# A ninth block-product pair for the first head pair's queries and keys, and the convolution's norm spread over units and value tiles

## The chip, the cores and the metric

One core of one Trainium2 chip runs the whole layer as one program. The metric is the device time of one launch in microseconds (us), the median of several launches; lower is better. Engines are named as in the profile: PE (matrix multiply; PEld is its weight load), DVE (vector), ACT (scalar), POOL (GpSimd), SP (queues most transfers).

## The reference, cut to what matters

One encoder layer over 1024 tokens of width 1024, in float32, output (1, 1024, 1024):

```python
proj = x @ w_in[l] + b_in[l]                      # 1024 x 4608: GLU input | q | k | v | branch gates
glu_in, q, k, v, gate_logits = jnp.split(proj, splits, axis=-1)
# conv_branch
u = a * jax.nn.sigmoid(gate)                      # then a causal depthwise conv of width 31
u = jax.nn.silu(layer_norm(u, ln_g, ln_b))        # layer norm over the 512 channels
y_conv = u @ w_out
y_attn = chunked_attention(heads(q), heads(k), heads(v), rel_bias[l]) @ w_attn_out[l]   # 8 heads of 64
g_conv, g_attn = jnp.split(jax.nn.sigmoid(gate_logits), N_BRANCHES, axis=-1)
mixed = (g_conv * y_conv + g_attn * y_attn) @ w_o[l] + b_o[l]
x = layer_norm(ALPHA * x + mixed, ...)            # then a grouped mixture of 16 experts, top 2, and a last norm
```

## The kernel before, in words

Every float32 product is made from three passes over operands that are split in a high and a low part (`mm3`, L685 to L687). ACT makes the high part of a weight block (`high`), POOL or DVE the low part (`low`). Channels lie on partitions, tokens along the free axis; a block is 128 output channels.

The work of PE runs through these stages, in the order of the PE program:

1. **GLU blocks** 0 to 7 (`weights_left`). Beside them DVE makes the GLU (`glu`) and the first of 124 convolution taps (`conv_tap`, each 128x1024 in the PSUM banks 6 and 7); SP loads the first unit weights into slots of the ring as blocks are used up (`load_unit`).
2. **Units.** The 16 gate blocks are made in 8 pairs (a block of conv gates and one of attention gates). A pair is a 2x2 product of halves (tokens in 2 halves of 512, input channels in 2 halves of 512), and seven block products stand in for eight (`UNITS`, `gate_product`, order `1, 6, 5, 7, 2, 3, 4`). A unit is 12 matmuls of 512 columns into one of six banks, 56 units in all. Four of the seven products of a pair need sums of weight halves: POOL issues those as transfers that accumulate in DRAM (`sums_round`, `weight_sums`), in rounds; the rounds 5 and 6 stand after the low part of units 4 and 9 (`LATE_ROUNDS`). DVE adds the products into `gst` (`gate_sums`, 7 sums a pair) and does one or two taps between them. ACT does the sigmoids and SP stores the gates. A unit waits until the bank of the unit six before it has been read (`bank_read`).
3. **Conv mean and value tiles.** `conv_mean` (L745) sums the channels by a matmul with ones. Then 8 value tiles for heads 0 to 3 (24 matmuls of 256 columns each) in four banks, with `conv_var` (L753) ahead of tile 5. On DVE: `centre` (L1367, 4 times), `square_sum`, and `v_low` (L1354) of each tile, which needs ACT's `v_high` (L1084) of that tile; then four reciprocals (L1376) and four `normalise` (L1349). ACT: four squares, `v_high`, a square root, the high parts of two blocks, four Silu (L1111).
4. **Queries and keys of the first head pair**: blocks 10 and 11, 96 matmuls of 512 columns into banks 0 to 3; ACT and DVE turn them into `qh`, `ql`, `kh`, `kl` (`qk_high`, `qk_low`).
5. **Attention**, 32 slots (`scores_of_slot`, `weigh_values`), with the queries and keys of the later head pairs and the rest of the values in between; then the output products, the norm and the experts, which the diff doesn't touch.

All engines run their programs in order. POOL's order in stage 3 is: low parts of blocks 8 to 11, two bias scalings (`scale_bias`, L609), low parts of blocks 12 and 13, then attention.

Of the kernel before, what the change touches and what calls it, by code (L numbers as in the profile page):

```python
# [39 lines left out]
VAR_TILE = 5  # L40
CCE_ROW = 2048
FIRST_UNITS = 4
LATE_ROUNDS = {4: 5, 9: 6}
# [6 lines left out]
B_V = (8, 16)  # L50
B_Q = (10, 12, 14, 18)
B_OC, B_OA, B_WO = 20, 24, 28
N_BLOCKS = 36
W_GATE = N_BLOCKS

# [9 lines left out]
UNITS = [(x, q) for q in range(KC) for x in ORDER]  # L65
N_UNITS = len(UNITS)
GATES_STORED = 16 * KC // 2


def block_columns():  # L70

    a, g, q, k, v, gate = 0, 4, 8, 12, 16, 20
    cols = []
    for j in range(CB):
        cols += [a + j, g + j]
    cols += [v, v + 1, q, k, q + 1, k + 1, q + 2, k + 2, v + 2, v + 3, q + 3, k + 3]
    return cols, [gate + j for j in range(N_GATE)]
# [21 lines left out]
def encoder_layer(nc, xT, x, wblk, b_in, dw, dwb, lncg, lncb, relb, b_o, ln1_g, ln1_b,  # L99
# [3 lines left out]
    wsum_dram = nc.dram_tensor("gate_weight_sums", (4, KC, P * DC), F32, kind="Internal").ap()  # L103
    gate_dram = nc.dram_tensor("gate_cols", (N_GATE, P, SEQ), F32, kind="Internal").ap()
    ctx = ExitStack()
    with ctx:
# [197 lines left out]
        def wait_used(eng, n):  # L304
# [3 lines left out]
            elif n < B_V[0]:  # L308
                eng.wait_ge(blk_used, B_V[0] + N_UNITS - 2 * (B_V[0] - 1 - n))
            elif n in B_V or n - 1 in B_V:  # L310
                eng.wait_ge(v_done, TT * (1 + (n >= B_V[1])))
            elif n < B_OC:
                b, i = [(b, n - B_Q[b]) for b in range(PAIRS) if 0 <= n - B_Q[b] < 2][0]
                eng.wait_ge(qk_done, 1 + max(p for p in range(4 * PAIRS) if qk_of(p)[:2] == (b, i)))
# [17 lines left out]

        def sum_round(x, q):

            return q // 2 + {5: 1, 7: 1, 6: 2, 3: 3}[x]

        def sums_issued(r):

            return sum(2 * many for g in range(KC // 2) for stage, many in enumerate((4, 2, 1, 1)) if g + stage <= r)
# [15 lines left out]
        def sigmoids_at(m):  # L355
# [3 lines left out]
            x, q = UNITS[m - 2]  # L359
            return [(q, slot) for after, slot in ((7, 3), (2, 0), (3, 2), (4, 1)) if after == x]  # L360
# [7 lines left out]
        V_BANKS = (0, 1, 2, 3)  # L368
# [53 lines left out]
        SPLITS = {1: (14,), 2: (15,), 5: (16,), 9: (17,), 13: (18,), 17: (19,), 25: (20,), 27: (21,), 29: (22,), 30: (23,),  # L422
                  31: (24,), 32: (25,), 33: (26,)}
# [41 lines left out]
        with nc.Block() as block:  # L465
            @block.sync
            def _(sp):
# [17 lines left out]
                def load_unit(m):  # L485

                    x, q = UNITS[m]
                    if m < UNIT_SLOTS:
                        sp.wait_ge(blk_used, B_V[0] - RING + m // 2 + 1)
# [5 lines left out]
                    sp.dma_start(uraw[:, m % UNIT_SLOTS], of.rearrange("(p k c) -> p k c", p=P, k=CB)).then_inc(u_in[m % UNIT_SLOTS], 16)  # L495
# [30 lines left out]
                for m in range(N_UNITS):  # L526
                    if m + UNIT_SLOTS < N_UNITS:
                        load_unit(m + UNIT_SLOTS)
                    elif m % 2:
# [8 lines left out]
                for n in range(B_V[0] + RING, B_WO):  # L538
# [4 lines left out]
                    if n == B_OA - 2:  # L543

                        sp.wait_ge(qk_done, 4 * PAIRS)
# [36 lines left out]
            def _(pool):  # L582
# [38 lines left out]
                def weight_sums(g, stage):  # L621

                    if not 0 <= g < KC // 2:
                        return
                    for q in (2 * g, 2 * g + 1):
# [10 lines left out]
                def sums_round(r):  # L636
# [3 lines left out]
                    for stage in range(4):  # L640
                        weight_sums(r - stage, stage)

                def unit_low(m):

                    s = m % UNIT_SLOTS
# [37 lines left out]
            def _(pe):  # L683
# [34 lines left out]
                def gate_product(m):  # L718

                    x, q = UNITS[m]  # L720
                    s, bank = m % UNIT_SLOTS, unit_bank(m)
# [26 lines left out]
                def conv_var():  # L748
                    bank_read(N_UNITS - 2)
                    bank_read(N_UNITS - 1)  # L750
                    pe.wait_ge(sum_ok, 2 * (CB - 1))
                    for h in range(2):
                        last = pe.matmul(ps[:, 4 + h, :], ones[:], sqr[:, 0, HALF * h:HALF * h + HALF], start=True, stop=True)  # L753
# [140 lines left out]
                def qk_sum(p, part, between=None, first=3):  # L894

                    b, i, h = qk_of(p)
                    if part == 0:
                        pe.wait_ge(w_lo, B_Q[b] + i + 1)
                        if p == 5:
                            pe.wait_ge(cent, CB)  # L900
                        elif p not in (4, 15):
# [114 lines left out]
            def _(act):  # L1016
# [11 lines left out]
                def unit_high(m):  # L1028
                    act.wait_ge(u_in[m % UNIT_SLOTS], 16 * (m // UNIT_SLOTS + 1))
                    act.activation(uh[:, m % UNIT_SLOTS], uraw[:, m % UNIT_SLOTS], ACT.Copy).then_inc(u_hi, 1)  # L1030
# [38 lines left out]

                for m in range(N_UNITS + 2):  # L1070
# [6 lines left out]
                    for q, slot in sigmoids_at(m):  # L1077
                        gate_sigmoid(q, slot)

# [6 lines left out]
                def qk_high(i, o):  # L1086
# [4 lines left out]
                    act.wait_ge(qk_done, i + 1)  # L1091
                    act.activation(dst[:, HALF * h:HALF * h + HALF], o, ACT.Identity,
                                   bias=b_in_t[:, col:col + 1]).then_inc(qk_hi, 1)

                for j in range(CB):
                    act.wait_ge(cent, j + 1)
                    act.activation(sqr[:, j, :], cv[:, j, :], ACT.Square).then_inc(sq_done, 1)
                for t in range(TT):
                    v_high(0, t, ps[:, V_BANKS[t % 4], 0:2 * P])
                    if t == 1:  # L1100
                        high(B_Q[0])
                    if t == 3:
                        high(B_Q[0] + 1)
                    if t == VAR_TILE:
                        act.wait_ge(stat_done, 2)
                        act.activation(std[:], psf[:, 4 * HALF:6 * HALF], ACT.Sqrt, scale=1.0 / DC, bias=eps[:]).then_inc(sq_done, 1)
                high(B_Q[1])
                high(B_Q[1] + 1)
                for j in range(CB):
                    act.wait_ge(nrm, j + 5)  # L1110
                    act.activation(cv[:, j, :], cv[:, j, :], ACT.Silu, scale=cpar[:, 1, j:j + 1],  # L1111
                                   bias=cpar[:, 2, j:j + 1]).then_inc(silu_done, 1)
                for i in range(4):
                    qk_high(i, ps[:, i, :])
# [96 lines left out]
            def _(dve):  # L1211
# [49 lines left out]
                def first_low(m):  # L1261
                    dve.wait_ge(u_hi, m + 1)
                    dve.tensor_tensor(ul[:, m], uraw[:, m], uh[:, m], ALU.subtract).then_inc(u_lo, 1)
# [45 lines left out]

                sums_made = [0]  # L1310
# [29 lines left out]
                glu(CB - 1)  # L1340
# [3 lines left out]
                assert taps == CB * CW  # L1344
# [11 lines left out]
                def qk_low(i, o):  # L1356
# [5 lines left out]
                    dve.scalar_tensor_tensor(out=lo[b % 2][:, c], in0=o, scalar=b_in_t[:, col:col + 1],  # L1362
                                             in1=hi[b % 2][:, c], op0=ALU.add, op1=ALU.subtract).then_inc(qk_lo, 1)

                dve.wait_ge(stat_done, 1)
                for j in range(CB):
                    dve.scalar_tensor_tensor(out=cv[:, j, :], in0=psf[:, 6 * HALF:8 * HALF], scalar=-1.0 / DC, in1=cv[:, j, :],  # L1367
                                             op0=ALU.mult, op1=ALU.add).then_inc(cent, 1)
# [1094 lines left out]
```

## Time and profile before

| what | value |
| --- | --- |
| time before, median of 3 runs | 1120.44 us (1118.47 to 1121.39) |
| time of the profiled execution | 1120.55 us |
| its span | 1118.8 us, granted clock 0.987 on average |
| PE, DVE, ACT, POOL busy | 97%, 74%, 50%, 33% of the span |
| units, from the first to the last | 95.4 to 253.6 us |
| conv mean and value tiles | 254.9 to 281.6 us |
| first queries and keys | 282.6 to 304.5 us |

A row of the timeline reads: start, duration, engine, line, operation, output <- inputs, shape, xcount (rows of one kind that follow each other are merged), and in brackets the idle time before it with what ended it. Durations of matmuls overlap: the time from one start to the next is the pace.

### The profile page before, as it was taken

The page shows a single profiled execution, that of the slowest core. Times are in us where ns is not written, and L with a number is a line of the kernel's source. Part 1 is how long each engine was busy: PE and PEld are TensorE (multiplying, and loading weights), DVE is VectorE, ACT ScalarE, POOL GpSimd, SP SyncE. Part 2 cuts the span into 40 slices and gives each one's busy share as a digit, 9 for nine tenths or more (in the row PEclk, how much of TensorE's full clock was granted, in tenths as well). Part 3 has the DMA queues.
Part 4 walks back from the last instruction along what each step waited for, and adds up shares of the span by engine and source line. Part 5 has one row for each costly group of instructions (what it writes and reads, how often), then busy time and mean ns, then how long its engine had stood idle before and what let it go on. Part 6 is the DMA issues. An engine that isn't in the chain of part 4 may idle for free.

```text
span 1118.8 us, 17230 instructions
## 1 busy us (share of the span) xinstructions
PE 1081.1 (97%) x5487; PEld 897.1 (80%) x5488; DVE 833.2 (74%) x1195; ACT 556.9 (50%) x854; POOL 365.0 (33%) x317
## 2 busy tenths in 40 slices
PE   9999999999999999999999999899999999999984
PEld 7887888888788889788888888788888888888762
DVE  7899999995667766666774688888588646548766
ACT  6412343434476755645330224487487545548764
POOL 2535454444176854667000000024122121112220
PEclk9998999999999999999999999999999999999998
DMA  9898555543201100450750435898999975699966
GB/s 324 252 232 192 162 161 147 159 145 104 75 20 43 31 33 7 183 225 23 269 188 1 157 149 204 304 329 313 377 325 365 317 250 183 205 382 327 348 206 243
DMA packets 60938, 222.68 MB, mean 199 GB/s; under 512 B 9169, under 2 KB 9553, under 8 KB 56770
## 3 DMA queue, kind: packets, MB, share of 16 engines
q1 hardware_dynamic: 51602, 182.49, 44.0%
q0 software_dynamic: 9264, 39.27, 14.5%
q8 instruction: 40, 0.66, 0.2%
q14 instruction: 32, 0.26, 0.1%
HBM read 189.27 MB, written 49.30 MB: 213 GB/s over the span
## 4 chain that ended last, share of the span: by engine, by line
PE 81%; DVE 6%; DMA 4%; ACT 3%; issue 3%; POOL 2%; DVEq 1%; ACTq 0%; SPq 0%; POOLq 0%
PE ps L685 15%; PE ps L687 15%; PE ps L686 15%; PE ps L1823 8%; PE ps L1825 8%; PE ps L1824 8%; PE ps L807 2%; PE ps L793 2%; DMA dn_raw<-in_wexp 2%; DMA gu<-in_wexp 2%; PE ps L779 2%; PE ps L1904 1%; PE ps L1819 1%; POOL pr L597 1%; PE ps L1931 1%
## 5 line engine op out<-in xcount | busy, mean ns | idle before, releaser
L1722 DVE TENSOR_TENSOR gu<-gu (+1 forms) x128 | 148.5, 1219 | 34.7 <-issue 20.8
L1245 DVE SCALAR_TENSOR_TENSOR ps<-u,dw_t,ps 128x1024 f32<-128x1024 f32 x116 | 149.1, 1285 | 2.3
L1823 PE MATMUL ps<-gu,xgh 128*128 x336 | 134.0, 399 | 3.4 <-DVE xgl L2221 2.8
L1716 ACT ACTIVATE gu<-gu (+1 forms) x128 | 124.0, 1047 | 21.7 <-DMA gu<-in_wexp 13.6
L1825 PE MATMUL ps<-gu,xgl 128*128 x336 | 131.7, 392 | 0.0
L1824 PE MATMUL ps<-gu,xgh 128*128 x336 | 131.4, 391 | 0.0
L597 POOL TENSOR_SCALAR pr<-pr,rinv 128x640 f32<-128x640 f32 (+4 forms) x64 | 95.4, 1503 | 77.3 <-DVE rinv L1407 77.1
L685 PE MATMUL ps<-xh,wh 128*128 128x512 f32 x256 | 102.9, 402 | 1.7 <-DVE vhl L1354 1.0
L686 PE MATMUL ps<-xl,wh 128*128 128x512 f32 x256 | 100.0, 390 | 0.0
L687 PE MATMUL ps<-xh,wl 128*128 128x512 f32 x256 | 99.8, 390 | 0.0
L647 POOL TENSOR_TENSOR ul<-uraw,uh 128x512 fp32r<-128x512 f32 x52 | 68.6, 1436 | 71.4 <-ACT uh L1030 71.4
L2316 DVE TENSOR_TENSOR dn_l<-dn_raw,dn_h 128x1024 fp32r<-128x1024 f32 x60 | 69.5, 1219 | 10.9 <-ACT dn_h L2064 10.8
L1823 PEld LDWEIGHTS ps<-gu,xgh 128*128 128x128 f32 x336 | 63.4, 189 | 17.4 <-issue 4.8
L1825 PEld LDWEIGHTS ps<-gu,xgl 128*128 128x128 f32 x336 | 63.4, 189 | 13.5
L1824 PEld LDWEIGHTS ps<-gu,xgh 128*128 128x128 f32 x336 | 63.6, 189 | 12.7
L1823 PE MATMUL ps<-dn_h,hbh 128*128 128x512 f32 x168 | 68.3, 407 | 2.4 <-DVE hbl L2320 2.4
L1760 POOL DMA_INDIRECT acc_rows<-ys,to_now x20 | 37.6, 1880 | 94.0 <-ACT ys L2089 77.6
L1825 PE MATMUL ps<-dn_h,hbl 128*128 128x512 f32 x168 | 66.6, 397 | 0.0
L1824 PE MATMUL ps<-dn_l,hbh 128*128 128x512 f32 x168 | 66.5, 396 | 0.0
L1120 ACT ACTIVATE pr<-pr,nmx 128x640 f32<-128x640 f32 (+4 forms) x64 | 44.1, 690 | 43.8 <-DVE nmx L1398 43.8
L1747 POOL COPY id_now<-ids_i 128x1 int32 (+1 forms) x19 | 11.3, 594 | 164.9 <-PE ps L1904 164.9
L2064 ACT ACTIVATE dn_h<-dn_raw 128x1024 fp32r<-128x1024 f32 x60 | 58.7, 1048 | 8.9 <-DMA dn_raw<-in_wexp 5.2
(308 smaller groups left out, 2662.3 us busy)
## 6 DMA issues: line engine op xcount, KB each, us to landing
gu<-in_wexp SPq DMA_DIRECT2D x64, 1024.0 KB, 8.8
dn_raw<-in_wexp SPq DMA_DIRECT2D x16, 2048.0 KB
raw<-in_wblk SPq DMA_DIRECT2D x36, 512.0 KB, 4.3
gate_weight_sums<-in_wblk POOLq DMA_DIRECT2D x48, 256.0 KB, 6.2
uraw<-gate_weight_sums SPq DMA_DIRECT2D x32, 256.0 KB, 2.9
gate_cols<-gst SPq DMA_DIRECT2D x32, 256.0 KB, 3.3
uraw<-in_wblk SPq DMA_DIRECT2D x24, 256.0 KB, 2.9
xf<-acc_rows SPq DMA_DIRECT2D x8, 512.5 KB, 8.3
```

The source lines that it names most:

```text
L597: pool.tensor_scalar(pr[n % 3][:, h, 0:nt * P], pr[n % 3][:, h, 0:nt * P], rinv[:, n % 3, h:h + 1], None, ALU.mult).then_inc(p_ready, 1)
L647: pool.tensor_tensor(ul[:, s], uraw[:, s], uh[:, s], ALU.subtract).then_inc(u_lo, 1)
L685: pe.matmul(o, a_h, b_h, start=first, stop=False)
L686: pe.matmul(o, a_h, b_l, start=False, stop=False)
L687: return pe.matmul(o, a_l, b_h, start=False, stop=last)
L1245: dve.scalar_tensor_tensor(out=so_far if k < CW - 1 else cv[:, j, :], in0=tap, scalar=w, in1=so_far, op0=ALU.mult, op1=ALU.add).then_inc(c ...
L1716: eng.activation(gu[:, par, k, 0, :], gu[:, par, k, 1, :].bitcast(F32), ACT.Copy).then_inc(gu_hi, 1)
L1722: eng.tensor_tensor(gu[:, par, k, 1, :], gu[:, par, k, 1, :].bitcast(F32), gu[:, par, k, 0, :], ALU.subtract).then_inc(gu_lo, 1)
L1823: pe.matmul(o, a_h, b_h, start=first, stop=False)
L1824: pe.matmul(o, a_h, b_l, start=False, stop=False)
L1825: return pe.matmul(o, a_l, b_h, start=False, stop=last)
L2316: dve.tensor_tensor(dn_l[:, k, :], dn_raw[:, k, :], dn_h[:, k, :], ALU.subtract).then_inc(dn_lo, 1)
```

## The change

- The gates' pairs become nine: `N_PAIRS = KC + 1`. Blocks `q` and `k` of the first head pair are stored like a gate pair and made by seven units, numbers 56 to 62. `B_Q[0]` and its 96 matmuls go; block numbers after it fall by two.
- The weight sums of the ninth pair are made in rounds 7 to 10, after the low part of units 14, 18, 22 and 26.
- The first unit sits in slot 1 of the ring in place of slot 0 (`FIRST_SLOT`), so that units 1, 3 and 5 are loaded one block later.
- `glu(CB - 1)`, the last GLU, moves up in DVE's program, ahead of the low parts of units 2 and 3 and of three taps.
- The mean goes ahead of unit 59 on PE; the four `centre` follow the gate sums of units 59 and 60 on DVE, the four squares come at steps 60 and 61 on ACT, the square sums after units 61 and 62 on DVE.
- `conv_var` goes ahead of value tile 1. The square root comes after `v_high` of tile 1; reciprocals stand at tiles 1 to 4, `normalise` and Silu at tiles 4 to 7; `qk_high` and `qk_low` at tiles 0 to 3, reading `gst` in place of PSUM (the keys with one pass more on ACT, for their sign).
- PE waits for all eight `v_low` before attention. On POOL both bias scalings now stand behind the low parts of the blocks 10 and 11, which ACT splits at tiles 3 and 4.
- The blocks of `w_o` are stored in another order (`in_ring`), since they start at another place of the ring.

```diff
-LATE_ROUNDS = {4: 5, 9: 6}
+LATE_ROUNDS = {4: 5, 9: 6, 14: 7, 18: 8, 22: 9, 26: 10}
+NORM_UNITS = 4
-UNITS = [(x, q) for q in range(KC) for x in ORDER]
+UNITS = [(x, q) for q in range(N_PAIRS) for x in ORDER]
+FIRST_SLOT = -N_UNITS % UNIT_SLOTS
+        FROM_SLOT = (0, 2, 1, 3)
+        V_BANKS = (1, 2, 3, 4)
...
# PE
                 for m in range(N_UNITS):
+                    if m == N_UNITS - NORM_UNITS:
+                        conv_mean()
                     gate_product(m)
-                conv_mean()
...
-                    if t == VAR_TILE:
+                    if t == 1:
                         conv_var()
                     v_tile(0, t, ps[:, V_BANKS[t % 4], 0:2 * P])
-                for i in range(2):
-                    pe.wait_ge(w_lo, B_Q[0] + i + 1)
-                    pe.wait_ge(v_lo, TT)
-                    for h in range(2):
-                        half_sum(B_Q[0] + i, h, ps[:, 2 * i + h, :], 0, KC).then_inc(qk_done, 1)
+                pe.wait_ge(v_lo, TT)
+                pe.wait_ge(sq_done, CB + 1)
# ACT
+                    if m in (N_UNITS - NORM_UNITS + 1, N_UNITS - NORM_UNITS + 2):
+                        square(2 * (m - N_UNITS + NORM_UNITS - 1))
+                        square(2 * (m - N_UNITS + NORM_UNITS - 1) + 1)
...
                 for t in range(TT):
                     v_high(0, t, ps[:, V_BANKS[t % 4], 0:2 * P])
                     if t == 1:
-                        high(B_Q[0])
+                        act.wait_ge(stat_done, 2)
+                        act.activation(std[:], psf[:, 6 * HALF:8 * HALF], ACT.Sqrt, scale=1.0 / DC, bias=eps[:]).then_inc(sq_done, 1)
+                    if t < 4:
+                        qk_high(t, gst[:, 0, FROM_SLOT[t], :])
                     if t == 3:
-                        high(B_Q[0] + 1)
...
+                        high(B_Q[1])
+                    if t == 4:
+                        high(B_Q[1] + 1)
+                    if t >= 4:
+                        j = t - 4
+                        act.wait_ge(nrm, j + 5)
+                        act.activation(cv[:, j, :], cv[:, j, :], ACT.Silu, scale=cpar[:, 1, j:j + 1],
+                                       bias=cpar[:, 2, j:j + 1]).then_inc(silu_done, 1)
# DVE
                     some_taps(TAPS_A_STEP // 2)
+                    if n == B_V[0] - 1:
+                        glu(CB - 1)
...
-                glu(CB - 1)
                 for m in range(N_UNITS):
                     gate_sums(m)
                     some_taps(1 + (m % 2 or m < 12))
+                    if m in (N_UNITS - NORM_UNITS, N_UNITS - NORM_UNITS + 1):
+                        centre(2 * (m - N_UNITS + NORM_UNITS))
+                        centre(2 * (m - N_UNITS + NORM_UNITS) + 1)
+                    if m == N_UNITS - NORM_UNITS + 2:
+                        square_sum(1)
+                        square_sum(2)
+                square_sum(3)
...
                 for t in range(TT):
-                    if 1 <= t <= 3:
-                        square_sum(t)
                     v_low(0, t, ps[:, V_BANKS[t % 4], 0:2 * P])
-                dve.wait_ge(sq_done, CB + 1)
-                for i in range(4):
-                    c = slice(2 * P * i, 2 * P * i + 2 * P)
-                    dve.reciprocal(rstdc[:, c], std[:, c]).then_inc(nrm, 1)
-                for j in range(CB):
-                    normalise(j)
-                for i in range(4):
-                    qk_low(i, ps[:, i, :])
+                    if t < 4:
+                        qk_low(t, gst[:, 0, FROM_SLOT[t], :])
+                    if 1 <= t <= 4:
+                        dve.wait_ge(sq_done, CB + 1)
+                        c = slice(2 * P * (t - 1), 2 * P * t)
+                        dve.reciprocal(rstdc[:, c], std[:, c]).then_inc(nrm, 1)
+                    if t >= 4:
+                        normalise(t - 4)
# POOL
-                for n in range(B_V[0], B_Q[0] + 2):
+                for n in range(B_V[0], B_Q[1] + 2):
                     low(n)
                 scale_bias(0)
                 scale_bias(1)
-                for n in range(B_Q[1], B_Q[1] + 2):
-                    low(n)
```

## Rows read from the trace of the kernel before

**Rows 1.** The page: each engine's busy time, share and instructions.
```profile
PE 1081.1 (97%) x5487; PEld 897.1 (80%) x5488; DVE 833.2 (74%) x1195; ACT 556.9 (50%) x854; POOL 365.0 (33%) x317
```
**Rows 2.** Timeline of PE: start us, us, line, operation, [idle before <-releaser].
```profile
95.38 0.39 PE L685 MATMUL ps<-xh,uh 128*128 128x512 f32 x1
...
98.10 0.39 PE L685 MATMUL ps<-xraw_r,uh 128*128 128x512 f32 x1
...
103.68 0.77 PE L685 MATMUL ps<-t_h,uh 128*128 128x512 f32 x1 [2.70 <-issue]
...
253.35 0.39 PE L687 MATMUL ps<-xraw_r,ul 128*128 128x512 f32 x1
254.93 1.96 PE L745 MATMUL ps<-csum,ones 128*128 128x512 f32 x4 [1.18 <-DVE csum L1253]
256.32 0.69 PE L685 MATMUL ps<-wh,xh 128*128 128x256 f32 x1
...
282.64 0.47 PE L685 MATMUL ps<-xh,wh 128*128 128x512 f32 x1 [1.03 <-DVE vhl L1354]
...
304.58 0.33 PE L779 MATMUL ps<-kh,qh 64*128 64x128 f32 x2
```
**Rows 3.** Stretches: length, busy us of PE, PEld, DVE, ACT, POOL, PEclk, DMA share, GB/s.
```profile
100.00:112.00 12.00, 9.30 (x29) 7.13 (x28) 11.86 (x11) 2.39 (x4) 8.62 (x10) 0.72 0.92 209
688.00:696.00 8.00, 7.87 (x48) 7.01 (x49) 6.54 (x29) 4.08 (x6) 1.09 (x1) 0.79 0.27 83
```
**Rows 4.** Timeline of ACT and of DVE around the last GLU.
```profile
95.58 1.12 ACT L1049 ACTIVATE sig<-ps,b_in_t 128x1024 f32<-128x1024 f32 x1 [6.49 <-PE ps L687]
...
97.26 1.28 DVE L1263 TENSOR_TENSOR ul<-uraw,uh 128x512 fp32r<-128x512 f32 x2
...
102.30 1.28 DVE L1229 SCALAR_TENSOR_TENSOR u<-ps,b_in_t,sig 128x1024 f32<-128x1024 f32 x1
```
**Rows 5.** Timeline of DVE: the two gate sums at unit 17.
```profile
154.50 1.41 DVE L1289 TENSOR_TENSOR gst<-ps,gst 128x512 f32<-128x512 f32 x2
```
**Rows 6.** Timeline of POOL: low parts of units 5 to 9, behind round 5.
```profile
106.33 7.40 POOL L647 TENSOR_TENSOR ul<-uraw,uh 128x512 fp32r<-128x512 f32 x5
```
**Rows 7.** Timeline of DVE from the value tiles to the first scores.
```profile
268.08 1.21 DVE L1259 TENSOR_TENSOR sqr<-sqr 128x1024 f32<-128x1024 f32 x1
...
282.07 0.43 DVE L1354 TENSOR_TENSOR vhl<-ps,vhl 128x256 fp32r<-128x256 f32 x1 [2.45 <-ACT vhl L1084]
282.41 6.58 DVE L1376 RECIPROCAL rstdc<-std 128x256 f32<-128x256 f32 x4
...
299.97 0.75 DVE L1362 SCALAR_TENSOR_TENSOR kl<-ps,b_in_t,kh 128x512 fp32r<-128x512 f32 x1 [0.85 <-ACT kh L1092]
```
**Rows 8.** The four `normalise` as one line of code: shortest, middle and longest in ns.
```profile
L1349 DVE TENSOR_TENSOR cv<-cv,rstdc x4: 1210/1211/3398, 289.0 to 294.6; 128x1024 f32<-128x1024 f32 x4
```
**Rows 9.** Timeline of ACT in the same stretch.
```profile
276.30 1.28 ACT L1106 ACT_TABLE_LOAD   x1
...
278.77 0.39 ACT L1084 ACTIVATE vhl<-ps 128x256 fp32r<-128x256 f32 x1
...
285.36 1.06 ACT L1020 ACTIVATE wh<-raw 128x1024 fp32r<-128x1024 f32 x1 [3.33 <-DMA raw<-in_wblk]
...
292.45 4.65 ACT L1111 ACTIVATE cv<-cv,cpar 128x1024 f32<-128x1024 f32 x4 [3.47 <-DVE cv L1349]
```
**Rows 10.** Timeline of POOL: bias scaling, then low parts of two blocks.
```profile
276.44 3.45 POOL L609 TENSOR_SCALAR bias<-bias 128x1280 f32<-128x1280 f32 x1
...
286.57 4.76 POOL L603 TENSOR_TENSOR wl<-raw,wh 128x1024 fp32r<-128x1024 f32 x2 [6.17 <-ACT wh L1020]
```
**Rows 11.** Timeline in attention: one DVE operation between two inputs of SBUF, and POOL's scalings.
```profile
460.67 2.67 DVE L1215 TENSOR_TENSOR wl<-raw,wh 128x1024 fp32r<-128x1024 f32 x1
...
462.24 2.80 POOL L597 TENSOR_SCALAR pr<-pr,rinv 128x256 f32<-128x256 f32 x2
...
356.03 1.83 POOL L597 TENSOR_SCALAR pr<-pr,rinv 128x256 f32<-128x256 f32 x2 [4.71 <-DVE rinv L1407]
```

More of the change, by code:

```diff
@@ L75, in block_columns @@
         cols += [a + j, g + j]
[L76 to L77 removed]
+    cols += [v, v + 1, q + 1, k + 1, q + 2, k + 2, v + 2, v + 3, q + 3, k + 3]
+    return cols, [gate + j for j in range(N_GATE)] + [q, k]
 C_ID, C_TRI, C_IOTA, C_TOK, C_THR, C_SPARE, C_EARLIER, C_SLOT, C_UPTO = 0, 128, 256, 388, 396, 404, 405, 421, 456
@@ L331, in gate_weights, with first_round, pairs_of, unit_slot @@
             return whole[P * DC * k:P * DC * k + P * DC]
+        SUM_GROUPS = (N_PAIRS + 1) // 2
+        def first_round(g):
+            return g if g < KC // 2 else KC // 2 + 3
+        def pairs_of(g):
+            return min(2, N_PAIRS - 2 * g)
+        def unit_slot(m):
+            return (m + FIRST_SLOT) % UNIT_SLOTS
         def sum_round(x, q):
-            return q // 2 + {5: 1, 7: 1, 6: 2, 3: 3}[x]
+            return first_round(q // 2) + {5: 1, 7: 1, 6: 2, 3: 3}[x]
         def sums_issued(r):
-            return sum(2 * many for g in range(KC // 2) for stage, many in enumerate((4, 2, 1, 1)) if g + stage <= r)
+            return sum(pairs_of(g) * many for g in range(SUM_GROUPS) for stage, many in enumerate((4, 2, 1, 1)) if first_round(g) + stage <= r)
         U2, W, U3, C22, C11, C12, C21 = range(1, 8)
@@ L621, in weight_sums @@
                 def weight_sums(g, stage):
-                    if not 0 <= g < KC // 2:
+                    if not 0 <= g < SUM_GROUPS:
                         return
-                    for q in (2 * g, 2 * g + 1):
+                    for q in range(2 * g, 2 * g + pairs_of(g)):
                         s1, s2, s3, s4 = (wsum_dram[i, q] for i in range(4))
@@ L639, in sums_round @@
                         pool.wait_ge(wsum_in, 16 * sums_issued(r - 1))
-                    for stage in range(4):
-                        weight_sums(r - stage, stage)
+                    for g in reversed(range(SUM_GROUPS)):
+                        if 0 <= r - first_round(g) < 4:
+                            weight_sums(g, r - first_round(g))
                 def unit_low(m):
-                    s = m % UNIT_SLOTS
+                    s = unit_slot(m)
                     pool.wait_ge(u_hi, m + 1)
@@ L748, in conv_var @@
                 def conv_var():
-                    bank_read(N_UNITS - 2)
-                    bank_read(N_UNITS - 1)
                     pe.wait_ge(sum_ok, 2 * (CB - 1))
                     for h in range(2):
-                        last = pe.matmul(ps[:, 4 + h, :], ones[:], sqr[:, 0, HALF * h:HALF * h + HALF], start=True, stop=True)
+                        last = pe.matmul(ps[:, 6 + h, :], ones[:], sqr[:, 0, HALF * h:HALF * h + HALF], start=True, stop=True)
                     last.then_inc(stat_done, 1)
@@ L1068, in gate_sigmoid, with square @@
                                    bias=b_in_t[:, 20 + 2 * q + n:21 + 2 * q + n]).then_inc(sig_ready, 1)
+                def square(j):
+                    act.wait_ge(cent, j + 1)
+                    act.activation(sqr[:, j, :], cv[:, j, :], ACT.Square).then_inc(sq_done, 1)
                 for m in range(N_UNITS + 2):
@@ L1308, in gate_sums, with centre @@
                         add(C21, 1, o, 1)
+                def centre(j):
+                    dve.wait_ge(stat_done, 1)
+                    dve.scalar_tensor_tensor(out=cv[:, j, :], in0=psf[:, 6 * HALF:8 * HALF], scalar=-1.0 / DC, in1=cv[:, j, :],
+                                             op0=ALU.mult, op1=ALU.add).then_inc(cent, 1)
                 sums_made = [0]
@@ L2431, in halves_apart, with in_ring @@
         return b.reshape(-1, P, 2, CB * P).transpose(0, 2, 1, 3).reshape(-1, P, KC, P)
+    def in_ring(i):
+        return i if i < 4 else 4 + (B_WO + i) % RING
     first, gates = block_columns()
     w_in = columns(w_in)
-    blocks = np.concatenate([w_in[first], two_a_block(w_conv_out), two_a_block(w_attn_out), columns(w_o), halves_apart(w_in[gates])])
+    blocks = np.concatenate([w_in[first], two_a_block(w_conv_out), two_a_block(w_attn_out), columns(w_o)[[in_ring(i) for i in range(KC)]], halves_apart(w_in[gates])])
     rel = np.clip(np.arange(P)[:, None] - np.arange(BANDW)[None, :] + 512, -256, 256) + 256
```

88 lines of the change are left out of this document (42 added, 46 removed).

## Prediction

> **What bounds the kernel now.** I read the page first. PE is busy 97% of the span and DVE 74% [rows 1], so a change pays where it takes matmuls away from PE or closes one of its gaps. Then PE's timeline from the units to the first scores [rows 2]. The first unit starts at 95.38 and the second at 98.10, so a unit takes 2.72 us and one matmul of 512 columns 0.227. At that pace 56 units would end at 95.38 + 56 x 2.72 = 247.7. The last one ends at 253.35 + 0.23 = 253.6. The 5.9 us between sit at unit 2: PE is idle 2.70 us until 103.68, and the granted clock of the stretch from 100 to 112 is 0.72 [rows 3]. PE's first matmul after the gap starts right behind DVE's last GLU (102.30 + 1.28 = 103.58) [rows 4], so the gap is that GLU's lateness, and 5.9 - 2.7 = 3.2 us are the price of the half clock (1.2 in place of 2.4 GHz) behind it. The other gaps are 1.18 ahead of the mean and 1.03 ahead of the first queries [rows 2]. Attention starts at 304.58.
>
> **First part: the last GLU.** Its sigmoid ends at 96.70, and DVE reaches the new place of the GLU at 97.26 [rows 4], so it ends at about 98.5, ahead of unit 2 at 95.38 + 2 x 2.72 = 100.8. The two low parts behind it end at 99.7, in time for units 2 and 3. The 5.9 us go. What is late next is DVE: its own program is as long as before, so its sums stay where they are while PE is earlier. The nearest call is the bank of unit 16, which is free when the second of the two sums at unit 17 ends, 154.50 + 1.41 = 155.91 [rows 5]; unit 22 uses it and would start at 155.2. With a semaphore's way that is a wait of 0.9; bounds 0 (if DVE gains a little) and 3 (if the clock falls again as at unit 2). I take 0.9, as the row gives it. The pair's later banks have 1 us or more to spare. Gain: 5.0.
>
> **Second part: seven units for 96 matmuls.** 96 x 0.227 = 21.8 go and 7 x 2.72 = 19.0 come: gain 2.7. DVE gets seven sums of 0.7 more, where taps have run out (the last comes at unit 54), at no cost. Six more copies and sums in DRAM, on POOL behind units 14 to 26, add at most 2 us to POOL at a place where it is several units ahead: 0. So are the changed slots (units 1, 3, 5 loaded one block later, two blocks ahead of use) and the new order of w_o: 0, bounds 0 and 1.2.
>
> **Third part: the mean inside the units.** The last column sum is made four units before the mean: the 1.18 go. The squares must be added up by value tile 1. Before, from the mean (256.32) to the last square sum (268.08 + 1.21) went 13.0 us [rows 2, 7]; now four units and one tile, 10.9 + 3.0 = 13.9, stand between, with three units' sums in between: a wait of 0.4, bounds 0 and 1.5.
>
> The value tiles then start at 95.38 + 63 x 2.72 + 1.39 (the mean) + 0.9 = 269.0. They take as long as before, 281.61 - 256.32 = 25.3 with the variance's matmuls [rows 2], and 0.4: PE has made the eighth at 294.7.
>
> **Fourth part, where I expect the gain to go: the chain between ACT and DVE.** Before, reciprocals, norm and Silu lay beside 96 matmuls of queries and keys (282.6 to 304.5). Now they lie between the value tiles, and PE may not start attention before the eighth v_low. Both engines run in order. From tile 4 on a step is v_high(t), v_low(t), normalise(t-4), Silu(t-4), and v_high(t+1) stands behind that Silu: four operations, none beside another. That is 0.38 + 0.43 + 1.21 + 1.16 with the signals some 3.3 us [rows 7 to 9], against 2.9 of PE for a tile. The chain also starts late. Tile 1 ends at 276.7; v_high, table load and square root (276.30 to 278.77 before, 2.5) end at 279.5 [rows 9]. DVE then does three qk_low of 0.72 (estimated from 0.75 in [rows 7]), four reciprocals of 1.65 and three v_low of 0.35 (pace) before normalise(0), which is ready at 290.0. From there three rounds of normalise, Silu, v_high and v_low lead to the eighth v_low at about 299.5: PE idles 4.8 us even if nothing else disturbs.
>
> POOL disturbs. Of four normalise one took 3.40 in place of 1.21 us [rows 8]: it began at 289.0, while POOL's second low part ran from 288.95 to 291.3 [rows 10], and it ended 1.1 after that. At 460.67 the same kind of operation took 2.67 and ended 1.1 after POOL's at 462.26; the two scalings of POOL behind it took 2.80 in place of 1.83 [rows 11]. So an operation of DVE on two SBUF operands and one of POOL exclude each other, to the end of the one running. In the new order POOL has, from 285.2 when ACT has split block 10: low 2.4, low 2.4, scaling 3.45, two memsets, scaling 3.45 [rows 10], that is until 298. In that time fall qk_low(3) (at 285.2, a tie with POOL), normalise(0) and normalise(1). If POOL wins the tie: qk_low(3) starts at 287.6, normalise(0) is ready at 291.9 and waits for the first scaling to 294.2; Silu, v_high and v_low of tile 5 bring normalise(1) to 297.3, which waits for the second to 298.8; two undisturbed steps bring the eighth v_low to 305.2. If DVE wins: normalise(0) at 290.8 behind the second low part, normalise(1) at 295.5, normalise(2) at 300.2, and the eighth v_low at 303.4. I take the middle, 304.3: 9.6 us of idle PE, and attention 0.3 us earlier than before. Bounds 299.5 and 306.
>
> The Trainium skill, page "SBUF — State Buffer", section "Who interferes with whom", says that a DVE instruction with two SBUF inputs contends with every GpSimd instruction that reads SBUF, and that the first one holds the ports to its end. The trace agrees for low parts and, by 2.80 against 1.83, for scalings. Were scalings exempt, the sum would be 2.8 us lower.
>
> **Clock.** After the 2.7 us gap at unit 2 the half clock cost 3.2. Around 690 the clock of 8 us is 0.79 [rows 3], 3.4 us at half: 1.7. PE is busy without a gap behind 304.58, so what the clock takes counts. I take the middle, 2.4; bounds 0 and 3.5.
>
> **Sum**: -0.3 + 2.4 = +2.1. On the profiled execution's 1120.55 us that is 1122.7; that execution is 0.1 above the median, so 1122.6 on the scale of the runs shown. A difference of 0.3% (3.4 us) is about what a measurement of this kernel tells from none.
>
> **Rivals.**
>
> *A, the forecast.* Its own range is 1120.5 to 1125.5. Chance 0.53.
>
> *B, the chain without waits for POOL, or with few.* DVE and POOL may meet otherwise than worked out, since a shift of 0.5 us moves an operation into a gap. The eighth v_low is at 299.5 to 301.5: attention starts 5.1 to 3.1 earlier, less 2.4 for the clock: 1117.8 to 1119.9. For it: three of four normalise were undisturbed [rows 8]. Against: POOL was idle then, and here it has 13 us without a gap. Chance 0.22.
>
> *C, the chain doesn't bind.* Attention starts at 294.7: 9.9 less, 1110.7. Against it stands the order of both programs. Chance 0.05.
>
> *D, the gap at unit 2 only moves (slower).* The low part of unit 5 stands behind round 5 of the weight sums, which waits for transfers. It ends at 106.33 + 7.40 / 5 = 107.8 [rows 6], and PE, now on time, wants it at 95.38 + 5 x 2.72 = 109.0. From a round 1.2 us later PE waits, and from a gap like that of unit 2 the clock falls again: up to 2.7 + 3.2 = 5.9 of the 5.9 come back. For it: three first unit loads now share the queues with that round. Against: a round's end was set by its own transfers. With it the time is 1124.5 to 1128.5. The same price has a first part that doesn't do what it says, because DVE's lag on PE grows beyond a bank. Chance 0.20.
>
> **Range and chances.** Low 1115.5 (B whole, a part beyond), high 1127.5 (most of D). Faster by over 0.3% (under 1117.1): C 0.05 and the third of B in which the clock takes less, 0.13 together. Slower by over 0.3% (over 1123.8): 0.18 of D and the upper fifth of A, 0.30. Within: 0.57.
>
> **What would show it.** The first part: no gap of PE at 101 and clock 1.00 from 100 to 112, unit 55 ended at about 249. The second: 63 units of 2.72. The fourth: PE idle for 9 to 10 us after the last value tile, released by DVE's L1354 line, normalise of over 2 us twice in four, a granted clock of half when scores begin, and first scores at 303.5 to 305.5. It is wrong if PE goes from value tiles to scores with under 4 us of idle time, if the clock stays at 1.00 there, or if a new gap stands in the units.

## The result, and the profile after

| | before | after |
|---|---|---|
| median of the runs timed together | 1120.49 us (1118.47 to 1121.39, 6 runs) | 1129.96 us (1128.24 to 1131.95, 6 runs) |
| ratio of after to before, 95% interval | | 1.008 (1.0065 to 1.0095) |
| profiled execution, its span | 1120.55, 1118.8 us | 1128.24, 1126.4 us |

The change makes the kernel 0.8% slower. The forecast was 1122.6 with a range up to 1127.5: the sign is right, and the time lies above the range. The page's line for after [rows 1]: PE is 2.0 us less busy and 9.6 us more idle.

```profile
PE 1079.1 (96%) x5475; PEld 895.2 (79%) x5476; DVE 836.9 (74%) x1202; ACT 560.5 (50%) x862; POOL 376.9 (33%) x330
```

Up to the first scores PE's timeline of after reads as the forecast worked it out. No gap stands at unit 2 any more, where before has 2.70 [rows 2]; the value tiles start at 269.04 (forecast 269.0), the last of their matmuls is issued at 294.37, and then PE idles 9.90 us until the eighth `v_low`. Columns: start, us, line, operation, [idle before <-releaser].

```profile
101.12 0.39 PE L708 MATMUL ps<-t_h,ul 128*128 128x512 f32 x1
...
269.04 0.28 PE L706 MATMUL ps<-wh,xh 128*128 128x256 f32 x1
...
294.37 0.28 PE L708 MATMUL ps<-wh,xl 128*128 128x256 f32 x1
304.55 0.47 PE L798 MATMUL ps<-kh,qh 64*128 64x128 f32 x2 [9.90 <-DVE vhl L1395]
```

DVE's timeline shows the chain that sets the 304.55. From the second `normalise` on, each round is `normalise`, an idle time in which ACT makes Silu and `v_high`, and `v_low`:

```profile
286.01 2.80 DVE L1404 TENSOR_TENSOR kl<-gst,kh 128x512 fp32r<-128x512 f32 x1
...
292.44 2.82 DVE L1390 TENSOR_TENSOR cv<-cv,rstdc 128x1024 f32<-128x1024 f32 x1
296.84 0.42 DVE L1395 TENSOR_TENSOR vhl<-ps,vhl 128x256 fp32r<-128x256 f32 x1 [1.57 <-ACT vhl L1106]
297.18 2.18 DVE L1390 TENSOR_TENSOR cv<-cv,rstdc 128x1024 f32<-128x1024 f32 x1
300.94 0.42 DVE L1395 TENSOR_TENSOR vhl<-ps,vhl 128x256 fp32r<-128x256 f32 x1 [1.57 <-ACT vhl L1106]
301.28 1.22 DVE L1390 TENSOR_TENSOR cv<-cv,rstdc 128x1024 f32<-128x1024 f32 x1
304.07 0.42 DVE L1395 TENSOR_TENSOR vhl<-ps,vhl 128x256 fp32r<-128x256 f32 x1 [1.57 <-ACT vhl L1106]
```

POOL's timeline in the same stretch, with the low parts and the scalings that fall on the three slow operations:

```profile
285.86 5.22 POOL L625 TENSOR_TENSOR wl<-raw,wh 128x1024 fp32r<-128x1024 f32 x2 [21.70 <-ACT wh L1035]
291.17 3.46 POOL L631 TENSOR_SCALAR bias<-bias 128x1280 f32<-128x1280 f32 x1
...
295.29 3.44 POOL L631 TENSOR_SCALAR bias<-bias 128x1280 f32<-128x1280 f32 x1
```

Stretches of after (length, busy us of PE, PEld, DVE, ACT, POOL, then PEclk, DMA share, GB/s). At unit 2 the clock is full where it was 0.72 [rows 3]; behind the value tiles it is half (1.2 GHz) through 14 us; and there is a new stretch near the end at 0.57:

```profile
100.00:112.00 12.00, 12.00 (x54) 9.94 (x53) 11.79 (x12) 3.08 (x5) 9.46 (x10) 1.00 1.03 272
297.00:311.00 14.00, 6.45 (x20) 4.71 (x22) 6.32 (x12) 6.42 (x10) 3.32 (x5) 0.51 0.15 60
1058.00:1070.00 12.00, 7.02 (x24) 5.33 (x23) 2.79 (x4) 3.07 (x5) 0.86 (x1) 0.57 0.24 102
```

Where the time went, by the distance of after from before: 0.0 at the first scores (304.55 against 304.58), +2.8 at the last (509.3 against 506.5) and at the first expert matmul (703.1 against 700.3), +1.4 at the last transposes' start behind the experts' loop (1057.73 against 1056.33), and +7.6 at the end of the span. So over 6 of the 7.6 us arise in the last 70 us, in code that the change doesn't touch. There PE's timeline of after shows the eight transposes of the last tile (`L1942`) broken in two:

```profile
1057.73 1.03 PE L1942 MATMUL ps<-ident_t,xg 128*128 128x128 f32 x6 [2.35 <-issue]
1063.26 0.58 PE L1942 MATMUL ps<-ident_t,xg 128*128 128x128 f32 x2 [4.49 <-issue]
1064.33 0.77 PE L1861 MATMUL ps<-dn_h,hbh 128*128 128x512 f32 x1 [0.49 <-issue]
...
1071.86 0.60 PE L1969 MATMUL ps<-ident_t,hb 128*128 128x128 f32 x4
```

In the kernel before, the same eight run in one piece:

```profile
1056.33 1.09 PE L1904 MATMUL ps<-ident_t,xg 128*128 128x128 f32 x8 [2.01 <-issue]
...
1063.00 0.60 PE L1931 MATMUL ps<-ident_t,hb 128*128 128x128 f32 x4
```

At the transposes behind that product (1071.86 against 1063.00) the kernel after is 8.9 us later: 7.5 of them arise in these 14 us, and over 1 comes back by the end.

"issue" means that PE waited for no semaphore that the profile shows. The traces hold one more thing that isn't data: a DMA queue of kind "instruction", q8, with loads of 16 KB. The starts of these loads around the loop's end, in us:

```
before      1048.0  1053.7  1059.5  1078.8
after       1049.4  1055.1  1061.0  1068.6
```

The load at 1061.0 is done at 1062.0, and PE goes on at 1063.26. The theory to test was therefore: behind the loop's last jump PE's instructions come in loads that follow one another by 5.8 us (the second and third start of each row), and in after the boundary between two of them falls among the transposes, because PE's program ahead of it is 20 instructions shorter (12 matmuls, each with its weight load, go; four waits come). Before, PE reaches that boundary only later. If a load is 256 instructions, 236 more do the same to the boundary as 20 fewer.

### The profile page after: what moved, and what is told of

Same layout as the page of the kernel before. It is cut to its first block, busy times and chain, and to the rows that moved or that the text cites. A ratio compares the mean times of both kernels' runs of the same rounds, so it can differ in the third digit from the quotient of the medians.

```text
span 1126.4 us, 17255 instructions
## 1 busy us (share of the span) xinstructions
PE 1079.1 (96%) x5475; PEld 895.2 (79%) x5476; DVE 836.9 (74%) x1202; ACT 560.5 (50%) x862; POOL 376.9 (33%) x330
## 4 chain that ended last, share of the span: by engine, by line
PE 82%; DVE 7%; DMA 4%; issue 2%; ACT 2%; POOL 2%; ACTq 0%; SPq 0%; POOLq 0%; DVEq 0%
PE ps L706 15%; PE ps L708 14%; PE ps L707 14%; PE ps L1861 9%; PE ps L1863 9%; PE ps L1862 9%; PE ps L826 2%; PE ps L812 2%; PE ps L798 2%; PE ps L1942 2%; DMA acc_rows<-ys,to_now 1%; PE ps L1857 1%; DMA dn_raw<-in_wexp 1%; PE ps L1969 1%; DMA xf<-acc_rows 1%
## 5 line engine op out<-in xcount | busy, mean ns | idle before, releaser
L670 POOL TENSOR_TENSOR ul<-uraw,uh 128x512 fp32r<-128x512 f32 x59 | 77.9, 1418 | 71.2 <-ACT uh L1045 66.8
L706 PE MATMUL ps<-xh,wh 128*128 128x512 f32 x224 | 91.4, 408 | 0.8 <-DVE xl L1247 0.5
L707 PE MATMUL ps<-xl,wh 128*128 128x512 f32 x224 | 88.4, 395 | 0.0
L708 PE MATMUL ps<-xh,wl 128*128 128x512 f32 x224 | 88.3, 394 | 0.0
L1798 POOL DMA_INDIRECT acc_rows<-ys,to_now x20 | 35.3, 1765 | 102.0 <-ACT ys L2127 72.3
L1082 ACT ACTIVATE gst<-gst,b_in_t 128x512 f32<-128x512 f32 x32 | 23.2, 724 | 85.3 <-DVE gst L1317 85.1
```

The costliest lines, as they stand in the source:

```text
L670: pool.tensor_tensor(ul[:, s], uraw[:, s], uh[:, s], ALU.subtract).then_inc(u_lo, 1)
L706: pe.matmul(o, a_h, b_h, start=first, stop=False)
L707: pe.matmul(o, a_h, b_l, start=False, stop=False)
L708: return pe.matmul(o, a_l, b_h, start=False, stop=last)
```

## The experiments

Each ratio is to the kernel before, timed on the same chip, with its 95% interval in brackets. The experiments ran on four chips, so between chips ratios are compared, not times. Dead instructions are instructions in a step that is never reached: they lengthen PE's program, and nothing executes them.

### Where instructions are loaded

**a_pad20: the kernel after with 20 dead instructions.**

```diff
# PE, in the experts' steps, in one that is never reached
+            if isinstance(i, int) and i == MAX_TILES - 2:
+                for _ in range(10):
+                    pe.matmul(ps[:, 5, :], hbh[:, 0:P], dn_h[:, 0, 0:HALF], start=True, stop=True)
```

> The changed kernel with 20 PE instructions more in a tile step of the experts that is never reached (so nothing more is executed), which puts PE's code behind the experts' loop back where it stood in the kernel before, modulo a 16 KB load of instructions. Theory I (the loss behind the last loop comes from where a load of PE instructions falls: 4.49 us of PE idle after six of eight transposes, and the half clock behind it): the gap is gone or as before (2.0 us), 1122 to 1125 us. Rival II (the loss comes from the experts' transfers, whose phase or addresses have changed): the gap stays, 1128 to 1132 us.

Measured: 1121.28 us, ratio 1.003 (1.0012 to 1.0048). Nothing executed differs from after, and 0.5% is gone (the time is 0.7 us below the theory's range). PE's timeline shows the transposes whole again, and the clock of the stretch behind them is full:

```profile
1057.24 1.09 PE L1942 MATMUL ps<-ident_t,xg 128*128 128x128 f32 x8 [2.13 <-issue]
...
1058.00:1070.00 12.00, 12.00 (x56) 9.46 (x54) 6.38 (x8) 8.70 (x12) 3.62 (x2) 1.00 0.21 87
```

**b_pad236: the kernel before with 118 such dead matmuls.**

> The kernel before with 236 PE instructions more in the same unreached step, which puts its code behind the loop where it stands in the changed kernel. Theory I: a gap of 4 to 5 us inside the transposes behind the loop, 1124 to 1128 us. Rival II: no such gap, 1119 to 1122 us.

Measured: 1125.92 us, ratio 1.005 (1.0032 to 1.0068). Its timeline has the break of after, at the same place, behind the sixth transpose, though nothing of the change is in it:

```profile
1056.65 0.87 PE L1904 MATMUL ps<-ident_t,xg 128*128 128x128 f32 x6 [2.17 <-issue]
1062.26 0.59 PE L1904 MATMUL ps<-ident_t,xg 128*128 128x128 f32 x2 [4.74 <-issue]
```

**a_pad128: after with 64 dead matmuls.**

> The kernel after with 128 TensorE instructions of dead code (64 matmuls) in the never reached step, in place of 20. Theory (the stall comes only when a boundary between two instruction loads of 256 falls into the first few microseconds behind the experts' loop): with 128, half a load further, the boundary lies far from there, so as with 20: about 1121 (1119.5 to 1122.5) and no wait over 3 us behind the loop. Rival (20 instructions give the old code position back, and only that one is good; any other shift costs): 1126 to 1131.

Measured: 1123.02 us (1119.31 to 1129.10), ratio 1.0038 (1.0015 to 1.0061). The transposes are whole (one wait of 2.28), so not only the old position is good. The time is 0.5 above the range expected, and the ten runs spread: seven from 1119.3 to 1124.8 and three above 1127. The profiled execution is one of the three. From 688 to 706, ahead of the experts, its clock is 0.53:

```profile
688.00:706.00 18.00, 18.00 (x83) 17.23 (x83) 10.68 (x42) 4.66 (x8) 1.09 (x1) 0.53 0.37 130
```

The dead code lies behind that place. The profiled execution of a_pad20, with the same code up to there, has 3.4 us of half clock around it where this one has 17.1, and two of a_pad20's ten runs are as long (1126.85, 1127.79), at a mean clock of 0.980 and 0.978 where the other eight have 0.982 to 0.988. So executions of the same code differ in their half clock. That it is this place which makes the two long runs of a_pad20 long isn't shown, as neither was profiled.

The loads of q8 say where PE crosses the next boundary. From the third of the starts listed above to the fourth go 7.2 to 7.5 us in the three kernels whose transposes break (after, b_pad236 and a_norm_behind below, each behind the sixth) and 17.3 to 20.9 us in the other eleven. PE's dead code alone moves them, so q8 serves PE. Shown by the three pad runs together: the position of PE's code costs a second wait of 4.5 to 4.7 us, with a clock of half behind it, and 5.6 us in all (0.8 less 0.3%, and 0.5% in b_pad236; the intervals allow some 3 to 8 us).

### What holds the first scores

**a_norm_behind: after, with the four `normalise` and Silu behind the value tiles.**

```diff
# ACT and DVE, in the loop over the value tiles
-                    if t >= 4:
-                        normalise(t - 4)       # on ACT: the Silu of t - 4
+                for j in range(CB):
+                    normalise(j)               # on ACT: the Silu of j
```

> The changed kernel with the four normalise on DVE and the four Silu on ACT moved from between the value tiles to behind them; nothing else. Theory (the chain between ACT and DVE holds PE 9.9 us at the end of the value tiles and costs 3 us more by the half clock): the eighth v_low comes at about 295, PE idles 1 to 4 us there, part of it in the first slots of attention, clock 1.00; first scores at 295 to 296, time 1121 to 1124 against 1130 of the changed kernel. Rival (the norm is on the path wherever it stands, since scores wait for it on DVE): the gap moves behind the first scores and the time stays at 1127 to 1130.

Measured: 1124.35 us, ratio 1.0042 (1.0024 to 1.006), where after has 1.008: nearly half of the loss is gone. First scores at 294.94 in place of 304.55, so `normalise` and Silu between `v_low` and `v_high` were the chain. A part of it comes back at the second scores, which wait for DVE's maxima behind 7.33 us of `normalise`:

```profile
294.94 0.33 PE L798 MATMUL ps<-kh,qh 64*128 64x128 f32 x2 [0.93 <-DVE vhl L1394]
302.60 0.58 PE L798 MATMUL ps<-kh,qh 64*128 64x256 f32 x2 [4.15 <-DVE nmx L1435]
```

**a_norm_behind_pad: that one with the 20 dead instructions.**

> The kernel after with two edits at once: the four normalises and four Silus behind the eight value tiles, and 20 TensorE instructions of dead code in a step that is never reached. Theory (the two losses are separate and add up: the chain behind the value tiles, and where TensorE's instruction loads fall behind the experts' loop): each edit keeps what it brought alone, 1129.96 to 1121.28 for the dead code (-8.7) and 1129.96 to 1124.35 for the order (-5.6), so 1129.96 - 8.7 - 5.6 = 1115.7; as the half clock behind the value tiles is in both savings in part (10.2 us of it in the one, 6.8 in the other, against 13.7), I expect 1116 to 1119, first scores at 294.9, and no wait of 4.5 us behind the experts' loop. Rival (what was saved at the value tiles is given back at the end of attention, as the convolution is late there): not under 1121.

Measured: 1117.52 us, ratio 0.9986 (0.9973 to 1.0). The two losses are separate and, within the intervals, add up: 1.0080 less 0.0050 (the dead code) less 0.0038 (the order) is 0.9992.

**a_scale_early: after with the 20 dead instructions, and POOL's scalings ahead of the low parts of blocks 10 and 11.**

```diff
# POOL
-                for n in range(B_V[0], B_Q[1] + 2):
+                for n in range(B_V[0], B_V[0] + 2):
                     low(n)
+                pool.wait_ge(v_hi, 1)
                 scale_bias(0)
                 scale_bias(1)
+                for n in range(B_Q[1], B_Q[1] + 2):
+                    low(n)
```

> The kernel after with the 20 dead instructions, and on GpSimd the two scale and bias operations ahead of the lows of units 10 and 11 (they start behind the first value tile's evictions). Theory (VectorE's first two normalises, 2.82 and 2.18 us, are stretched by GpSimd's work beside them, as the last two take 1.22): both come to about 1.22, the last v_low and the first scores 2.0 to 2.6 us earlier (about 301.8), time 1118.7 to 1119.5 against 1121.28 of the same kernel without the edit. Rival (they wait for something else, ScalarE's Silu order or TensorE's tile): durations stay over 2 us, or the scores stay at 304.2, time 1121 to 1122.

Measured: 1119.58 us, ratio 1.0011 (0.9999 to 1.0022); the median of the ratio is 0.19% (2.1 us) under a_pad20's 1.003, which was timed on another chip, and the intervals overlap. The traces carry it: the first scores come at 301.7 in place of 304.2, and the four `normalise` as one line of code (shortest, middle, longest in ns) are all of one length, first in this kernel, then in after:

```profile
L1393 DVE TENSOR_TENSOR cv<-cv,rstdc x4: 1215/1216/1226, 292.2 to 301.6; 128x1024 f32<-128x1024 f32 x4
```
```profile
L1390 DVE TENSOR_TENSOR cv<-cv,rstdc x4: 1215/1700/2823, 292.4 to 304.4; 128x1024 f32<-128x1024 f32 x4
```

### What the last GLU was worth

**b_glu_early: the kernel before with this edit alone.**

> The kernel before with the last GLU moved up as in the change; nothing else. Theory: the gap of 2.7 us at unit 2 and the half clock behind it go, and units end 5 to 5.9 us earlier; 1114.5 to 1116 us. Rival: DVE, whose program is no shorter, holds the units back, or the time is lost again further on: 1118 to 1121.

Measured: 1120.01 us, ratio 0.9996 (0.9976 to 1.0017). The theory's 1114.5 to 1116 missed, and the rival was right. The gap at unit 2 is gone, and the wait ahead of the mean is 3.57 where it was 1.18 [rows 2]: DVE, with as much to do, is late there instead.

```profile
251.21 1.96 PE L745 MATMUL ps<-csum,ones 128*128 128x512 f32 x4 [3.57 <-DVE csum L1253]
```

Its profiled execution, 1117.03 us, has the first scores at 300.9, and that of before at 304.58. But b_pad236, which keeps the gap (2.55), has them at 301.4, as its clock stays full behind it. So 0.5 of the 3.7 us are the gap less the longer wait, and 3.2 are a half clock that not every execution has.

**a_glu_late: after with the 20 dead instructions and the GLU back in its old place.**

> The kernel after with the 20 dead instructions, and the last GLU put back where the kernel before has it (behind the other evictions of the units' start). Theory of the prediction (that GLU is worth the gap of 2.7 at the second unit less 0.9 elsewhere, and in some executions the half clock with it): gap of about 2.5 at the second unit again and 2 to 5 us slower than the kernel with dead code alone, 1123.3 to 1126.5. Rival (the GLU's 1.23 us only trades places: the wait goes to the sums of the squares at the units' start, as in the run of that edit alone): within 1 us of 1121.28.

Measured: 1127.76 us (4 runs), ratio 1.0083 (1.0067 to 1.01) against 1.003: 0.53%, 5.9 us (the intervals allow some 3 to 9), 1.3 us above the theory's range. The gap is back, 3.4 us of half clock come behind it, and the first scores are at 308.8 in place of a_pad20's 304.2.

```profile
103.72 0.77 PE L706 MATMUL ps<-t_h,uh 128*128 128x512 f32 x1 [2.88 <-issue]
```

So the edit is worth 5.9 us where the mean stands inside the units (4.6 of them are there at the first scores), and nothing that the runs can tell where PE waits for DVE's sums ahead of the mean.

### A version that beats both

**v_silu_spread and v_silu_once: from a_norm_behind_pad, the `normalise` at attention's tiles 8 to 11, the Silus at tiles 12, 14, 16 and 18, or all four at tile 16.**

```diff
# ACT, at the end of attention's tile n
+                    for j in {12: (0,), 14: (1,), 16: (2,), 18: (3,)}.get(n, ()):
+                        silu(j)
# DVE, at the end of attention's tile n
+                    if 8 <= n < 8 + CB:
+                        normalise(n - 8)
```

> The kernel with the normalises behind the value tiles and the 20 dead instructions (1117.52), but each normalise at the end of VectorE's attention tiles 8 to 11, and each Silu at the end of ScalarE's attention tiles 12, 14, 16 and 18. Nothing reads the convolution's output before tile 23. Theory (ScalarE and VectorE have slack in attention, 12.4 and 13.5 of 20 us busy against TensorE's 19.4): TensorE's wait of 4.2 us at the second scores goes, and at least 3.4 of the half clock with it, while each Silu with its two table loads (1.22 + 2 x 1.28 = 3.8 us) costs TensorE at most 0.5: 1117.5 - 4.2 - 1.7 + 0 to 2 = 1111.5 to 1113.5, last scores about 498.5. Rival (what is not done at the value tiles comes back in attention in full): each of the four Silus stalls TensorE by 1 to 2 us, 1116 to 1119.

> As the one with the Silus spread over attention, but all four Silus together at the end of ScalarE's attention tile 16 (two table loads and 4.65 us, 7.2 us in one piece). Theory: the piece is longer than the exponentials' lead, so TensorE waits for probabilities once for 2 to 4 us there; 1113 to 1116, between the spread form and 1117.5. Rival (the lead, two tiles of some 6 us, covers it in whole): the same as the spread form or up to 1 us faster, as two table loads are fewer.

Measured: 1122.16 us, ratio 1.0023 (1.0009 to 1.0036), and 1122.36 us, ratio 1.0026 (1.0011 to 1.0041). My theory was wrong, and so was the size of its rival. The wait at the second scores went, and at tile 6 both kernels were 7.5 us ahead; between 320 and 420 they lost that and 3 more (last scores 507.2 against 504.2). Two stretches of a_norm_behind_pad, then of v_silu_spread:

```profile
320.00:360.00 40.00, 39.31 (x258) 33.00 (x257) 29.91 (x93) 26.77 (x65) 25.20 (x17) 1.00 0.11 39
360.00:420.00 60.00, 59.24 (x424) 51.97 (x423) 41.62 (x126) 36.48 (x88) 41.69 (x29) 1.00 0.09 30
```
```profile
320.00:360.00 40.00, 37.09 (x244) 30.92 (x243) 30.52 (x89) 26.06 (x63) 26.77 (x17) 1.00 0.13 44
360.00:420.00 60.00, 53.68 (x365) 46.11 (x365) 38.03 (x112) 46.38 (x89) 35.28 (x23) 0.97 0.06 21
```

Here ACT and DVE of a_norm_behind_pad are busy 60 to 75%, yet what was put into their idle time held PE up: from 310 to 510 its waits in v_silu_spread are 10.5 us in place of 2.7, all but 0.8 of them ended by DVE. That this idle time is many short waits for each other's results in one chain, which anything put between them lengthens, is the explanation that fits; no run tests it by itself. v_silu_once divides the loss: its lead over a_norm_behind_pad is 7.5 us from the third scores on, 3.2 at the scores of 391.0, with only `normalise` added so far, and behind its four Silus (from 392.1) it is 3.0 late at 409.8. So 4.3 us go along with `normalise` and 6.2 with the Silus and their table loads; how the 6.2 divide isn't settled.

**w_scale_early and w_norm_first: a_norm_behind_pad with POOL's scalings early as above; and with `normalise(0)` also ahead of the last `v_low`.**

```diff
# DVE (w_norm_first only)
+                    if t == TT - 2:
+                        normalise(0)
-                for j in range(CB):
+                for j in range(1, CB):
                     normalise(j)
```

> The kernel with the normalises and Silus behind the value tiles and the 20 dead instructions (1117.52), and GpSimd's two scale and bias operations ahead of the lows of units 10 and 11 (at 274 to 282). Theory (GpSimd's work beside them stretches VectorE's four normalises, 7.33 us in all where 4 x 1.22 is 4.9): the wait at the second scores falls from 4.2 to about 1.8, and up to 3.4 of the half clock with it: 1112.5 to 1115.5. Rival (as in the two kernels with the Silus in attention, what attention gains at its start it gives back by its end): TensorE's wait shrinks at the second scores, last scores stay at 504.2 within 0.7, 1117 to 1118.5.

> As the one before, and the first normalise ahead of VectorE's last v_low, in its wait of 2.09 us there. Theory: 1.22 us off the wait at the second scores again (about 0.6 left), first scores unmoved at 295: 1111.5 to 1114.5, 0 to 1.5 below the one before. Rival (the normalise holds up the last v_low, and the first scores with it): first scores up to 1.2 us later, time equal within 1 us.

Measured: 1115.24 us, ratio 0.9966 (0.994 to 0.9993), and 1113.81 us, ratio 0.9936 (0.9918 to 0.9954). The wait at the second scores is 1.46, then 0.35; the clock from 290 to 310 is 1.00 in both. Which of the two is faster their intervals don't tell; w_norm_first is 0.6% faster than before and, by the ratios, 1.4% faster than after (0.9936 against 1.008). Its timeline of PE:

```profile
295.63 0.33 PE L801 MATMUL ps<-kh,qh 64*128 64x128 f32 x2 [0.93 <-DVE vhl L1397]
299.45 0.39 PE L801 MATMUL ps<-kh,qh 64*128 64x256 f32 x2 [0.35 <-DVE nmx L1440]
304.49 0.44 PE L815 MATMUL ps<-ident_t,pr 128*128 128x128 f32 x2 [1.47 <-POOL pr L619]
```

## Why the prediction was wrong

**The step that failed is the sum's missing term for the end of the kernel.** The prediction carried attention's shift of +2.1 unchanged to the end and let only the clock around 690 vary; for code behind the change it counted nothing. There the shorter program of PE moved a load boundary among the last transposes: waits for "issue" there of 6.8 in place of 2.0 us, and a half clock (0.57 from 1058 to 1070). Dead code alone takes 5.6 us of the 9.0 away (0.8% to 0.3%). What is left, 0.3% or 3.4 us (1.3 to 5.4), agrees with the forecast's 2.1; the rest of the sum holds within what the runs can tell. The row that could have warned is the gap of 2.01 marked "issue" at 1056.33: it shows a fetch behind the jump, though not how near the next one was.

Point by point, by the traces:

- **First part.** Right in after: no gap, clock 1.00, and no wait at unit 22 (0.9 forecast): PE's only wait from 95 to 269 is 0.2. Undoing it costs 5.9 us. What I had not seen is that its worth hangs on the third part.
- **Second and third part.** Value tiles from 269.04 (269.0), PE through with the eighth at 294.65 (294.7). The variance's 0.49 stands for the 0.4.
- **Fourth part.** First scores at 304.55 (304.3), PE idle 9.90 (9.6). POOL won the tie at 285.9, `qk_low(3)` took 2.80, two `normalise` 2.82 and 2.18, the others 1.22. For a tie that POOL wins the forecast had worked out 305.2, with each of these waits longer; it took the middle of its two cases. The way ahead of them was somewhat longer instead (first `normalise` ready at 292.44, worked out for 291.9). So the 0.3 us between forecast and result are in part luck: errors of both signs.
- **The rule of the Trainium skill on the shared port** ("SBUF — State Buffer", "Who interferes with whom") holds for scalings too: once they lay earlier, the four `normalise` took 1.22 each and the scores came 2.5 us sooner, near the 2.8 of the prediction. What the rows don't show is a DVE operation held to the very end of POOL's: both stretched `normalise` end 0.6 us behind the scaling beside them (295.26 against 294.63, 299.36 against 298.73), and one takes 1.22. That is why the waits were shorter than forecast.
- **Clock.** 0.51 through 14 us, and the shift grew by 2.8 (2.4).
- **Rivals.** B and C didn't come about, as POOL's work fell where it hurt. D had the right price for a gap at unit 2 (5.9), but no gap came there. What it describes, a gap of PE and a half clock behind it, came 950 us later.

The Trainium skill, page "Runtime: NRT & Kernel Launch", section "Instruction fetch mechanics", says that instructions come in blocks of 16 KB, 256 each, ahead of use, that crossing a block boundary is mostly hidden, and that a taken branch out of the fetched part stalls. The traces agree on the 16 KB and, as 236 dead instructions do what 20 fewer do, on the 256; they agree on the stall behind the loop too, 2.0 to 2.5 us. They differ on the boundary: one in the straight code right behind the branch costs a second stall of 4.4 to 4.7.

## What to carry to other kernels

An edit that changes how many instructions an engine has moves its load boundaries in all the code behind: before a result is explained by the edit, run the same kernel with dead instructions that restore the old count. When, as ACT and DVE here, two engines pass work back and forth in program order, what stands between their steps can be on the path even with both partly idle; put it behind the last step that PE needs, and PE's next need ahead of as much of it as possible. A wait removed at one place is worth what no later wait takes back, so an edit's worth is measured in the kernel that it is meant for.

## What the runs showed of the hardware

- The two loads of PE's instructions behind the loop's last jump start 5.8 us apart in before (1053.7, 1059.5), 6.0 in after (1055.06, 1061.03) and 5.0 to 5.8 in the other twelve kernels, though one takes about 1 us. That a boundary can cost 4.4 to 4.7 us fits this; why they don't follow one another faster stays open.
- The clock behind much the same gap isn't the same in each execution. Behind the gap of 2.5 to 2.9 us at unit 2 it was half for 6.8 us in before, 3.4 in a_glu_late and never in b_pad236, whose code is that of before up to the experts and whose first scores come at 301.4 where before has 304.58. The 3.2 us that the prediction read there are those of one execution; how many executions have them isn't known.
